# Reordering the head loop of a differential-attention decoder step across TensorE, VectorE and ScalarE

## The chip, the cores and the metric

The kernel runs on one NeuronCore of a Trainium2 chip. The metric is the device time of one execution in microseconds (us). Engines are named as in the profile: PE is TensorE (matmul), PEld its weight load, DVE is VectorE, ACT is ScalarE, POOL is GpSimd, SP is SyncE, which issues most of the loads.

## The reference

It is one inference step of a two-layer decoder, for a prompt of 512 tokens and 8 requests of 4 new tokens each (544 token columns in all), in float32. The model width is 1024. Layer 0 mixes tokens by causal pooling; layer 1 uses differential attention with 6 heads, each with two sets of 64-wide queries and keys and 128-wide values. Both layers have a small memory attention and an MLP.

```
def diff_core(q, k, v, q_pos, k_pos, lam):
    s = jnp.einsum('bqhjd,bkhjd->bhjqk', q, k) * (DIFF_HEAD_DIM ** -0.5)
    s = jnp.where(mask[None, None, None], s, NEG_INF)
    p = jax.nn.softmax(s, axis=-1)
    a = p[:, :, 0] - lam * p[:, :, 1]
    return jnp.einsum('bhqk,bkhe->bqhe', a.astype(v.dtype), v)
...
o = rmsnorm(o, p['subln'][j]) * (1.0 - lam_init)
x = x + jnp.concatenate([mix, mem_out], axis=-1) @ p['w_out'][l]
h2 = rmsnorm(x, p['norm2'][l])
x = x + jnp.square(jax.nn.relu(h2 @ p['w_mlp1'][l])) @ p['w_mlp2'][l]
```

The change touches only `diff_core` for layer 1: 24 prompt items (6 heads times 4 query blocks of 128 rows; block i sees (i+1) x 128 keys) and the 8 requests, done two at a time against 256 cached keys and 32 new ones.

## The kernel before

The kernel is one block in which each engine has its own instruction stream, ordered by hand, and the streams meet only at semaphores. Most of the time goes to 186 weight units: a 128 x 1024 slab of weights is loaded, split into a high part (ACT, L807) and a rest (DVE, L1083), and multiplied in 48 matmuls (L445). Between the value projection and the output projection of layer 1 stands the head loop, `attention(FIRST_HEAD, len(ITEMS))`, which has no weight units in it.

The loop has 28 items, numbered 20 to 47. 24 are "diff" items, called here by their width w = i+1 from 1 to 4 (keys in blocks of 128); the widths run 1, 2, 3, 4 for each head. Four are "decode" items, numbers 28, 32, 37 and 43. Items 20 to 27 are the first two heads without a decode item. The steps of an item n are these:

- scores(n), PE: two products of queries and keys (L545), or for a decode item 24 + 12 short matmuls (L556, L560). It needs the exponentials of item n-3, since the scores have three pairs of PSUM banks.
- bias(n), DVE: adds the causal mask (L1183), takes the row maximum (L1190) and scales it (L1194); for a decode item L1187, L1192 and L1198. It needs scores(n).
- exponentials(n), ACT: one or two activations with row sums (L869). It needs bias(n) and the turn of item n-3.
- weights(n), DVE: reciprocal of the sums (L1159), a ratio (L1167) and the difference of the two softmaxes (L1169); for a decode item L1172 and L1173. It needs exponentials(n).
- turn(n), PE: w transposes of the weights into PSUM bank 6 (L582); a decode item uses matmuls (L585, L587). It needs weights(n) and, since there is one such bank, the copy of item n-1.
- copy(n), ACT: bank 6 to SBUF (L883; a decode item also L882). It needs turn(n).
- mix(n), PE: w products with the values into bank 7 (L620; decode L630). It needs copy(n) and the drain of item n-1.
- drain(n), DVE: bank 7 to SBUF (L1216). A decode item needs three steps between mix and drain: a copy to SBUF on ACT (L905), a decode turn on PE (L650, `decode_turn`), then six small copies on DVE (L1222).
- clamp and squares(n) on POOL (L1623) and ACT (L893, L895), for the norm behind the attention.

After item 42 DVE also computes factors of the first 16 rows of results (L1227 to L1230 and L1236) and scales four heads (L1242), for which ACT takes a square root (L912) and must change its table of functions twice. `mix_new` (L658) adds the new tokens' share near the end. SP issues the loads of the cached keys and values of a decode item (L389), keys after the scores of the decode item before, values after its decode turn.

The order of the three streams in one turn n of the loop is: on PE scores(n+2), decode turn(n-2), turn(n), mix(n-1); on ACT exponentials(n+1), decode copy(n-2), copy(n), squares(n-3); on DVE weights(n), drain(n-2), bias(n+2). The helpers are `scores` L518, `turn` L564, `mix` L591, `decode_turn` L646 (PE), `items_exp` L860, `items_copy` L873 (ACT), `items_weight` L1151, `items_bias` L1176, `items_drain` L1201 (DVE).

Of the kernel before, what the change touches and what calls it, by code (L numbers as in the profile page):

```python
# [105 lines left out]
def build(nc, xT, memT, hist, params, consts, ropes, weights, memK, memV, cacheK, cacheV, pages,  # L106
# [5 lines left out]
    with ctx:  # L112
# [201 lines left out]
        def probs(n):  # L314
            return Pr[2 if n >= FIRST_HEAD else int(n >= L0_ITEMS)][n % slots(n)]
# [17 lines left out]
        DECODE = [n for n, it in enumerate(ITEMS) if it[0] == "decode"]  # L333

        def decode_rows(n):

            return T[:, n % 2, 4 * GROUP:4 * GROUP + 3 * P]
# [89 lines left out]
        def _(pe):  # L427
# [136 lines left out]
            def turn(n):  # L564
                kind, a, i = ITEMS[n]
                l = int(n >= L0_ITEMS)
                t0 = 6
                pr = probs(n)
                pe.wait_ge(weighted, n + 1)
                if n >= 1:  # L570
                    pe.wait_ge(copied, n)
                if kind == "mem":
                    for kt in range(2):
                        for hh in range(2):
                            at = (2 * kt + hh) * P
                            mm = pe.transpose(ps[:, t0, at:at + P], pr[:, hh, lo_of(kt)], ident)  # L576
                elif kind == "memdec":
                    for kt in range(2):
                        mm = pe.transpose(ps[:, t0, lo_of(kt)], pr[:, 0, lo_of(kt)], ident)
                elif kind == "diff":  # L580
                    for kt in range(i + 1):
                        mm = pe.transpose(ps[:, t0, lo_of(kt)], pr[:, 0, lo_of(kt)], ident)  # L582
                else:
                    for kt in range(2):
                        pe.matmul(ps[:, t0, 2 * GROUP * kt:2 * GROUP * (kt + 1)], pr[:, 0, lo_of(kt)], C2[:, n % 2, :],  # L585
                                  start=True, stop=True)
                    mm = pe.matmul(ps[0:SAMPLE, t0, 4 * GROUP:6 * GROUP], pr[:, 0, PAST:PAST + SAMPLE], C2[:, n % 2, :],  # L587
                                   start=True, stop=True)
                mm.then_inc(turned, 1)
# [72 lines left out]

            def attention(n0, n1):

                for n in range(n0, n1):
                    if n + 2 < n1:
                        scores(n + 2)
                    if n - 2 in DECODE:
                        decode_turn(n - 2)
                    turn(n)  # L670
                    if n > n0:
                        mix(n - 1)
                    if n == n1 - 1:
                        mix_new(n)
                mix(n1 - 1)
# [122 lines left out]
        def _(act):  # L798
# [98 lines left out]

            def attention(n0, n1):
                items_exp(n0)
                for n in range(n0, n1 + 3):  # L900
                    if n + 1 < n1:
                        items_exp(n + 1)
                    if n - 2 in DECODE:
                        act.wait_ge(decode_mixed, DECODE.index(n - 2) + 1)
                        act.activation(decode_rows(n - 2), ps[:, 7, 0:3 * P], ACT.Copy).then_inc(decode_copied, 1)  # L905
                    if n < n1:
                        items_copy(n)
                    if n0 <= n - 3:
                        items_square(n - 3)
                    if n == EARLY_DONE + 2:  # L910
                        act.wait_ge(sub_mean, 1)
                        act.activation(rr[:, 0:EARLY], ss[:, 0:EARLY], ACT.Sqrt, bias=eps_sub, scale=SUB)\  # L912
                           .then_inc(sub_root, 1)
# [162 lines left out]
        def _(dve):  # L1076
# [168 lines left out]
            def attention(n0, n1):  # L1245
                items_bias(n0)
                items_bias(n0 + 1)
                for n in range(n0, n1 + 2):
                    if n < n1:
                        items_weight(n)  # L1250
                    if n - 2 >= n0:
                        items_drain(n - 2)
                    if n + 2 < n1:
                        items_bias(n + 2)
                    if n == EARLY_DONE + 1:
                        dve.wait_ge(squared, EARLY)
                        means(ss[:, 0:EARLY], ss_big[:, 0:EARLY], ss[:, 0:EARLY], rr2[:, 0:EARLY], keep[:, 0:EARLY])
                    if n == EARLY_DONE + 3:
                        head_factors(0, EARLY, 1)
                        for h in range(EARLY_HEADS):  # L1260
                            scale_head(h)
                dve.wait_ge(new_mixed, 1)
                dve.wait_ge(drained, DEC[-1] + 1)
                zs = Z[:, 0:MIXT, PROMPT:TOK]
                new = ps[:, 2 * ((n1 - 2) % SLOTS), 0:NS].rearrange("p (h t) -> p h t", h=MIXT)
                dve.tensor_tensor(zs, zs, new, ALU.add).then_inc(new_added, 1)
# [477 lines left out]
```

## Time and profile before

| what | us |
|---|---|
| median of 3 runs (lowest to highest) | 1279.95 (1279.94 to 1280.48) |
| the profiled execution, its own time | 1280.49 |
| its span, first to last instruction | 1278.5 |
| head loop, first scores to the start of the last turn of heads | 717.5 to 817.4 |
| PE busy in the whole span | 1220.1 (95%) |
| mean granted TensorE clock, share of full speed | 0.977 |

The head loop takes 100 of 1278 us. The profiled execution is 0.54 us above the median and its span is 2.0 us under its own time. A profile row of the timeline gives a start and a duration, and in square brackets how long the engine stood idle before it and what ended that.

### The profile page before, as it was taken

Reading aid. Unit: us, or ns where it says so; the run is one execution under the profiler, and the core shown is the slowest. Engines: PE = TensorE matmul, PEld = TensorE weight load, DVE = VectorE, ACT = ScalarE, POOL = GpSimd, SP = SyncE. Lnnn points to the kernel's source line nnn. Section 1 sums busy time; section 2 is a strip of 40 time slices with the busy share of each in tenths; the row PEclk is TensorE's granted clock in tenths of the full one; section 3 lists DMA queues with packets and bytes.
Section 4 is the critical chain, followed back from the end, with each engine's and each line's share of the span. In section 5 each row is a group of like instructions: output and inputs, shape, how many; then the busy total and the mean of one; then the engine's idle time right before and its main releaser. Section 6 shows DMA issues by size and latency. Waiting matters only on the chain.

```text
span 1278.5 us, 23202 instructions
## 1 busy us (share of the span) xinstructions
PE 1220.1 (95%) x9578; PEld 1169.1 (91%) x9578; DVE 581.7 (45%) x880; ACT 409.2 (32%) x756; POOL 346.9 (27%) x284
## 2 busy tenths in 40 slices
PE   6998999999999999999999898699999999999997
PEld 5877999999999999998899655599999999999997
DVE  7667444333333333446635867645333333333334
ACT  6545332212212212334412456533212212211221
POOL 3363115205205205320062200012511511511521
PEclk9999999999999999999999889699999999999998
DMA  7624322222322322232354546022232232232222
GB/s 281 210 85 128 119 83 87 96 83 83 99 84 83 97 85 83 83 93 75 132 135 119 197 156 214 1 66 79 90 97 83 83 99 83 83 99 84 84 66 71
DMA packets 38032, 132.97 MB, mean 104 GB/s; under 512 B 4178, under 2 KB 7122, under 8 KB 37298
## 3 DMA queue, kind: packets, MB, share of 16 engines
q1 hardware_dynamic: 36834, 123.42, 30.5%
q0 software_dynamic: 1104, 8.15, 2.1%
q8 instruction: 76, 1.25, 0.4%
q14 instruction: 18, 0.15, 0.0%
HBM read 121.18 MB, written 7.03 MB: 100 GB/s over the span
## 4 chain that ended last, share of the span: by engine, by line
PE 89%; DVE 7%; ACT 2%; issue 1%; DMA 0%; POOL 0%; DVEq 0%; SPq 0%; ACTq 0%
PE psum L445 80%; DVE weights_split L1083 1%; DVE inv_rms L1102 1%; PE psum L620 1%; ACT weights_split L807 1%; PE psum L531 1%; PE psum L545 1%; DVE tiny L1190 1%; PE psum L582 1%; PE psum L556 1%; PE psum L602 1%; PE psum L576 0%; PE psum L630 0%; PE psum L560 0%; PE psum L490 0%
## 5 line engine op out<-in xcount | busy, mean ns | idle before, releaser
L445 PE MATMUL psum<-operand_b,weights_split 128*128 128x272 f32 x4416 | 562.6, 289 | 4.1 <-DVE weights_split L1083 3.9
L445 PEld LDWEIGHTS psum<-operand_b,weights_split 128*128 128x128 f32 x4416 | 556.7, 189 | 9.1 <-DVE weights_split L1083 4.9
L445 PE MATMUL psum<-operand_a,weights_split 128*128 128x272 f32 (+1 forms) x4068 | 521.3, 290 | 21.4 <-DVE weights_split L1083 14.8
L445 PEld LDWEIGHTS psum<-operand_a,weights_split 128*128 128x128 f32 x4068 | 514.4, 190 | 27.7 <-issue 20.3
L807 ACT ACTIVATE weights_split<-weights_raw 128x1024 fp32r<-128x1024 f32 (+1 forms) x186 | 192.6, 1036 | 395.3 <-PE psum L445 395.3
L1083 DVE TENSOR_TENSOR weights_split<-weights_raw,weights_split 128x1024 fp32r<-128x1024 f32 (+1 forms) x186 | 239.5, 1288 | 136.6 <-ACT weights_split L807 136.5
L1506 POOL TENSOR_TENSOR squares<-staging 128x544 f32<-128x544 f32 x64 | 76.5, 1195 | 469.7 <-ACT operand_a L853 207.7
L1137 DVE TENSOR_TENSOR residual<-psum,residual 128x544 f32<-128x544 f32 x48 | 34.8, 725 | 176.0 <-PE psum L445 176.0
L1118 DVE SCALAR_TENSOR_TENSOR staging<-psum,inv_rms 128x544 f32<-128x544 f32 x56 | 40.6, 724 | 150.1 <-PE psum L445 150.1
L1499 POOL TENSOR_TENSOR squares_sum<-squares_sum,squares 128x544 f32<-128x544 f32 (+1 forms) x35 | 48.6, 1389 | 115.6 <-ACT squares L819 115.0
L1508 POOL TENSOR_TENSOR operand_a<-squares,operand_a 128x544 fp32r<-128x544 f32 x32 | 64.9, 2029 | 2.5
L1508 POOL TENSOR_TENSOR operand_b<-squares,operand_b 128x544 fp32r<-128x544 f32 x32 | 64.9, 2028 | 2.5
L853 ACT ACTIVATE operand_a<-staging 128x544 fp32r<-128x544 f32 x24 | 15.8, 658 | 109.9 <-DVE staging L1118 109.9
L853 ACT ACTIVATE operand_b<-staging 128x544 fp32r<-128x544 f32 x24 | 15.8, 658 | 109.8 <-DVE staging L1118 109.8
L1106 DVE TENSOR_TENSOR residual<-psum,residual 128x544 f32<-128x544 f32 x31 | 22.5, 724 | 58.8 <-PE psum L445 58.8
L1190 DVE TENSOR_REDUCE tiny<-psum 128x2 f32<-128x512 f32 (+3 forms) x40 | 30.8, 770 | 9.9 <-PE psum L531 8.9
L819 ACT ACTIVATE squares<-residual 128x544 f32<-128x544 f32 x39 | 25.2, 646 | 30.9 <-DVE residual L1106 30.9
L814 ACT ACTIVATE operand_a<-residual,params 128x544 fp32r<-128x544 f32 x16 | 12.0, 751 | 64.1 <-DVE residual L1106 64.1
L1499 POOL TENSOR_TENSOR squares_sum<-squares 128x544 f32<-128x544 f32 (+1 forms) x6 | 8.2, 1368 | 84.1 <-ACT squares L819 84.1
L883 ACT ACTIVATE staging<-psum 128x512 f32<-128x512 f32 (+4 forms) x48 | 22.4, 468 | 26.4 <-PE psum L582 22.3
L1623 POOL TENSOR_SCALAR squares<-attention_out 128x128 f32<-128x128 f32 x24 | 7.1, 294 | 87.2 <-DVE attention_out L1216 87.2
L814 ACT ACTIVATE operand_b<-residual,params 128x544 fp32r<-128x544 f32 x24 | 17.8, 740 | 37.7 <-DVE residual L1106 37.7
(209 smaller groups left out, 729.2 us busy)
## 6 DMA issues: line engine op xcount, KB each, us to landing
weights_raw<-in_weights SPq DMA_DIRECT2D x180, 512.0 KB, 3.6
cache_tiles<-in_page_k SPq DMA_DIRECT2D x16, 384.0 KB, 4.3
cache_tiles<-in_page_v SPq DMA_DIRECT2D x16, 384.0 KB, 3.9
cache_tiles<-in_mem_k SPq DMA_DIRECT2D x8, 512.0 KB, 4.6
cache_tiles<-in_mem_v SPq DMA_DIRECT2D x8, 512.0 KB, 5.2
residual<-in_x SPq DMA_DIRECT2D x1, 2176.0 KB, 11.5
rotated<-projected POOLq DMA_DIRECT2D x4, 408.0 KB, 7.0
rotated<-keys POOLq DMA_DIRECT2D x4, 408.0 KB, 7.6
```

Of the source, the lines that this page charges most:

```text
L445: mm = pe.matmul(ps[:, 2 * (j % PS) + hf, 0:n], w(wr), act[:, ar, k, hf * n:(hf + 1) * n], start=(q == 0 and wr == 0 and ar == 0), stop=(q ...
L807: act.activation(split[:, s % HL, 0, 0:n], raw[:, s, 0:n], ACT.Copy).then_inc(weight_hi, 1)
L814: act.activation(dst, src, ACT.Copy, scale=gain(g, k)).then_inc(norm_hi, 1)
L819: act.activation(SQ[:, k % 2, 0:cols], src, ACT.Square).then_inc(sq_ready, 1)
L853: act.activation(hidden[:, 0, j, :], T[:, j % TS, :], ACT.Square).then_inc(hid_hi, 1)
L1083: dve.tensor_tensor(split[:, s % HL, 1, 0:n], raw[:, s, 0:n], split[:, s % HL, 0, 0:n].bitcast(F32), ALU.subtract).then_inc(weight_lo, 1)
L1118: dve.scalar_tensor_tensor(out=halves(T[:, j % TS, :]), in0=unit_psum(j), scalar=0.0, in1=halves(rms[:, :]), op0=ALU.max, op1=ALU.mult).th ...
L1137: dve.tensor_tensor(halves(X[:, j, :]), unit_psum(j), halves(X[:, j, :]), ALU.add)\
L1190: own.chain(dve.tensor_reduce(mx[:, s, :], sc[:, :, 0:n_keys], AX.X, ALU.max))
L1499: pool.tensor_tensor(sq_sum[:, 0:cols], a, SQ[:, k % 2, 0:cols], ALU.add).then_inc(sq_summed, 1)
L1506: pool.tensor_tensor(sq, t, t, ALU.mult).then_inc(hid_sq, 1)
L1508: pool.tensor_tensor(hidden[:, 1, j, :], sq, hidden[:, 0, j, :].bitcast(F32), ALU.subtract)\
```

## The change

It alters only the order of steps in the three `attention` loops. On PE, the scores of item n+3 come between turn(n) and mix(n-1); the scores of item n0+2 are ahead of the loop. On ACT, the exponentials of item n+2 are ahead of copy(n) and behind the decode copy of n-2. On DVE, one turn of the loop is: drain of a decode item n-2, weights(n+1), bias(n+3), drain(n-1) if that is not a decode item. No operation is added or removed.

```
@@ PE
             def attention(n0, n1):
 
+                scores(n0 + 2)
                 for n in range(n0, n1):
-                    if n + 2 < n1:
-                        scores(n + 2)
                     if n - 2 in DECODE:
                         decode_turn(n - 2)
                     turn(n)
+                    if n + 3 < n1:
+                        scores(n + 3)
                     if n > n0:
                         mix(n - 1)
@@ ACT
                 items_exp(n0)
+                items_exp(n0 + 1)
                 for n in range(n0, n1 + 3):
-                    if n + 1 < n1:
-                        items_exp(n + 1)
                     if n - 2 in DECODE:
                         act.wait_ge(decode_mixed, DECODE.index(n - 2) + 1)
                         act.activation(decode_rows(n - 2), ps[:, 7, 0:3 * P], ACT.Copy).then_inc(decode_copied, 1)
+                    if n + 2 < n1:
+                        items_exp(n + 2)
                     if n < n1:
                         items_copy(n)
@@ DVE
                 items_bias(n0)
                 items_bias(n0 + 1)
-                for n in range(n0, n1 + 2):
-                    if n < n1:
-                        items_weight(n)
-                    if n - 2 >= n0:
+                items_weight(n0)
+                items_bias(n0 + 2)
+                for n in range(n0, n1 + 1):
+                    if n - 2 in DECODE:
                         items_drain(n - 2)
-                    if n + 2 < n1:
-                        items_bias(n + 2)
+                    if n + 1 < n1:
+                        items_weight(n + 1)
+                    if n + 3 < n1:
+                        items_bias(n + 3)
+                    if n > n0 and n - 1 not in DECODE:
+                        items_drain(n - 1)
                     if n == EARLY_DONE + 1:
```

## Rows read from the trace of the kernel before

**Rows 1.** Busy time by engine in the head loop; columns as in the first line.

```profile
core 0: us, PE busy (x) PEld busy (x) DVE busy (x) ACT busy (x) POOL busy (x), PEclk, DMA share, GB/s
717.00:818.00 101.00, 82.97 (x540) 54.07 (x541) 73.43 (x229) 59.17 (x241) 12.49 (x40) 0.84 0.52 180
```

**Rows 2.** What DVE waited for in the head loop: us in total, times, longest.

```profile
DVE projected L1222 <- PE psum L650: 8.4, 4, 2.7
DVE attention_out L1216 <- PE psum L620: 7.6, 5, 4.4
DVE psum L1187 <- PE psum L560: 3.6, 3, 1.9
DVE psum L1183 <- PE psum L545: 3.1, 6, 0.8
```

**Rows 3.** The same of PE.

```profile
PE psum L582 <- DVE probs_heads L1169: 8.0, 9, 2.5
PE psum L585 <- DVE combine L1173: 2.8, 3, 1.2
...
PE psum L620 <- DVE projected L1222: 1.2, 2, 0.6
```

**Rows 4.** Timeline around the turn of decode item 37: start, duration, what.

```profile
774.76 0.49 ACT L883 ACTIVATE staging<-psum 128x384 f32<-128x384 f32 x1 [1.07 <-PE psum L582]
...
776.09 0.16 DVE L1159 RECIPROCAL tiny<-tiny 128x1 f32<-128x1 f32 x1
...
776.21 0.69 ACT L869 ACTIVATE staging<-psum,tiny 128x512 f32<-128x512 f32 x1 [0.38 <-DVE tiny L1194]
...
776.72 0.34 DVE L1216 TENSOR_SCALAR attention_out<-psum,tiny 128x128 f32<-128x128 f32 x1
776.86 0.67 PE L585 MATMUL psum<-combine,probs_heads 128*128 128x80 f32 x4 [1.22 <-DVE combine L1173]
776.89 0.68 ACT L869 ACTIVATE staging<-psum,tiny 128x512 f32<-128x512 f32 x1
```

**Rows 5.** Durations by shape of exponentials and weights, widths 1 and 4.

```profile
L869 ACT ACTIVATE probs_heads<-psum,tiny 128x128 f32<-128x128 f32 x6 | 2.1, 350 | 0.0
...
L1169 DVE SCALAR_TENSOR_TENSOR staging<-staging,tiny 128x128 f32<-128x128 f32 x3 | 1.1, 351 | 0.1
```

**Rows 6.** Timeline of the mix, copy, turn and drain of decode item 32.

```profile
763.13 2.55 PE L630 MATMUL psum<-cache_tiles,staging 128*32 128x384 f32 x16
...
765.61 0.92 PE L545 MATMUL psum<-keys,projected 64*128 64x384 f32 x4
765.76 0.49 ACT L905 ACTIVATE staging<-psum 128x384 f32<-128x384 f32 x1 [0.43 <-PE psum L630]
766.46 0.55 PE L650 MATMUL psum<-constants,staging 128*128 128x128 f32 x3
...
767.04 0.53 DVE L1222 COPY projected<-psum 128x8 f32<-128x8 f32 x6 [2.71 <-PE psum L650]
...
767.49 0.42 DVE L1183 TENSOR_TENSOR psum<-psum,constants 128x256 f32<-128x256 f32 x1
```

**Rows 7.** Timeline of the mix and copy of decode item 28.

```profile
747.98 1.50 PE L630 MATMUL psum<-cache_tiles,staging 128*32 128x384 f32 x16
...
749.48 0.58 ACT L869 ACTIVATE probs_heads<-psum,tiny 128x384 f32<-128x384 f32 x1 [0.55 <-DVE tiny L1194]
...
750.61 0.49 ACT L905 ACTIVATE staging<-psum 128x384 f32<-128x384 f32 x1
```

**Rows 8.** Busy time and clock in three stretches of 2 us; columns as in rows 1.

```profile
728.00:730.00 2.00, 2.00 (x9) 1.12 (x9) 1.61 (x6) 0.96 (x5) 0.29 (x1) 0.50 0.97 397
...
748.00:750.00 2.00, 2.00 (x33) 0.96 (x34) 1.86 (x6) 1.37 (x7) 0.00 (x0) 1.00 0.02 4
...
762.00:764.00 2.00, 2.00 (x14) 1.11 (x16) 1.66 (x6) 0.76 (x3) 0.00 (x0) 0.50 0.94 333
```

**Rows 9.** Timeline, the last mix of the loop.

```profile
814.89 2.08 PE L620 MATMUL psum<-values,staging 128*128 128x128 f32 x8
```

## The prediction

> **What bounds the kernel now.** I read the busy time of the head loop first [rows 1]. In 101 us PE is busy for 83, DVE for 73 and ACT for 59, so no engine is full: PE and DVE wait for each other in turn. The lists of waits say where. DVE stood 22.7 us: 8.4 for four decode turns, 7.6 for mixes, 3.6 and 3.1 for scores of decode and diff items [rows 2]. PE stood 8.0 + 2.8 us for the weights [rows 3]. A reordering can win back only such waits. 4.35 of the 7.6 us belong to the very last drain, behind the last mix (2.1 us, at half clock), and nothing in the change touches that [rows 2, 9]. Outside the loop nothing moves.
>
> Written as one stream, the new order is less than its name. PE went turn(n), mix(n-1), scores(n+3), turn(n+1); it will go turn(n), scores(n+3), mix(n-1), turn(n+1). DVE went weights(n), drain(n-2), bias(n+2) and will go weights(n), bias(n+2), drain(n-2). So on both engines a step moves past one neighbour. The wait of scores(n+3) for exponentials(n) is met before turn(n) can run. Only on ACT does the order bite: exponentials(n+2) used to follow copy(n) and now precede it, although they need a bias that DVE makes only after weights(n). No operation is added, so a term has a price only where the step lies on the path; I cost each with two ends.
>
> **Term A, the scores come earlier by one mix.** Bias of diff items waited 3.1 us in six places, of decode items 3.6 us in three [rows 2]. The mix now moved behind is that of item n-1. I price a mix of w products from the last one: width 4, 2.08 us at half clock, so about 1.05 at full, and 0.3 to 1.0 by width (estimate from that row) [rows 9]. The six diff waits are 0.8 us at most [rows 2] and could vanish: 3.1. Of the three decode waits the mixes in front are widths 1, 4 and 1, so 0.35 + 1.05 + 0.35, about 1.8. Upper end 4.9 us gained. Lower end: the turn in front of those scores starts later (term B) and takes it all back, 0. The half of it is nearest to what a walk through the stream gives, since PE runs at half clock in part of the first two heads [rows 8] and is then late itself: I take 2.4 us gained.
>
> **Term B, the copy waits behind the exponentials.** From the end of bias(n+2), turn(n+1) used to need drain plus weights on DVE. It now also needs exponentials(n+2), then copy(n). For the turn of item 37 the rows carry all of it: exponentials of width 4 start at 776.21 and their second part ends at 777.57, so 1.37 us; the copy of width 3 is 0.49 us; that makes 1.86 us from 776.21, and 0.1 for the semaphore [rows 4]. On DVE from the same moment, drain and decode weights in the new order are 0.27 + 0.62, and the turn follows 0.14 later: the turn of 37 came at 776.86, where the copy would allow it at about 778.1 if bias stood where it stood [rows 4]. So this turn is about 1.0 us late. For diff turns the same sum gives less. Exponentials of width 1 are 2 x 0.35 us and copies 0.28 to 0.6 us, against 0.27 + weights of 0.8 (width 1, whose last operation is 0.35) to 1.2 us (width 4) [rows 4, 5]: the turns of widths 1 and 3 are late by 0.4 to 0.5, width 2 by 0.25, width 4 not at all. Diff turns are mostly covered, for bias(n+4) comes only after bias(n+3), a drain and weights, over 2.3 us later, and turn plus scores are 1.3 to 2.0 us at full clock. If that cover is gone, at half clock, each costs up to 0.5 us. The turns of decode items are not covered where PE stood waiting for the weights, as it did three times, 2.8 us [rows 3]. The longest was 1.2, so two of them make up at least 1.6 of it. I take two turns at 1.0 us plus 0.3: 2.3 us lost; ends 0 and 4.0 (four turns) plus some 2 us for diff turns.
>
> That ACT really holds the copy back is seen in the old trace. The mix of item 28 ended at 749.48, ACT was then only about to start exponentials that had waited 0.55 us for their bias, and the decode copy came behind them at 750.61 [rows 7]. The Trainium skill, page TensorE: Matmul & The Clock Gate, section on the array of 16 x 32x32, says ScalarE and VectorE work through their queues strictly in order while TensorE can at least pull weight loads ahead. The trace agrees for ACT: 1.13 us between the end of that mix and the copy. By that rule alone term B has no way round.
>
> **Term C, the decode items.** Before, the scores of a diff item (0.85 us) stood between a decode mix and its decode turn and hid the ACT copy of 0.49 us: mix ends 765.68, turn starts 766.46, drain 767.04 [rows 6]. After, the decode turn comes straight behind the mix and PE stands while ACT copies, 0.1 + 0.5 + 0.1 = 0.65 us, and the mix itself comes 0.85 later because the scores are now ahead of it. So a decode drain comes 0.65 later, 1.95 us over three items. What is gained is that the bias that stood behind the drain (it started at 767.49, 1.5 us long; 0.8 for one item) is done within the 2.7 us for which DVE waited anyway: 1.5 + 1.5 + 0.8 = 3.8 us. The mix that stood twice for the decode drain, 1.2 us, is covered by scores now [rows 3]. But between the decode items PE has hardly a gap, and where PE is the bound the DVE gain is idle: then the term is -1.95 + 1.2 = -0.75. Ends: 0.75 lost, 1.9 gained. I take 0, nearer the PE-bound end because all three decode drains end a stretch in which PE never stops.
>
> **Term D, the end.** Weights(45) and bias(47) move ahead of the scaling of four heads, and exponentials(45) ahead of ACT's change of table, so PE can do turn(45) before the block; yet drain 43 moves behind it and mix(44) waits for that drain. One more wait for scores, at most 0.8 us [rows 2], can go there, and one decode drain is no longer waited for, at most 0.65 (term C). Ends 0 and 1.45; I take 0.6 gained, under the middle since two moves there work against each other. The last two mixes and `mix_new` stay as they are: 0.
>
> Loads: the keys of item 37 and the values of item 32 are issued after steps that come within 1 us of where they came, and both were used some microseconds after landing, so 0; if that cover went, the scores of 37 would wait under 1 us. POOL's clamp and the squares follow a drain one bias later and are used three items on: 0.
>
> **Sum.** 2.4 - 2.3 + 0 + 0.6 = 0.7 us gained. The profiled execution would go from 1280.49 to 1279.8 and, the median being 0.54 lower, the time to about 1279.3. A measurement of this kernel can tell 0.2% from no change, 2.56 us, so this is no change.
>
> **Rivals.**
> 1. *The lead pays* (faster). If PE holds its full clock, term A is there whole, C near its upper end and B small: 4.9 + 1.0 - 2.3 + 1.0 = 4.6 us, 1275.3; half way, 1276.7. For it speaks that DVE's scores waits are short and each smaller than a mix. Against it, that PE runs at half clock in parts of the loop, mean 0.84 [rows 1], just where turns and scores would have to catch up.
> 2. *Copies behind exponentials become the bound* (slower). PE idles about 2 us ahead of turns 32 and 37 (the 1.2 of before and term B's 1.0, less what it did earlier) [rows 3, 4], and the diff turns at half clock pay 0.5 each. Price: B at 5, A at 1.5, C at -0.75, D at 0.6: 3.65 lost, 1283.6. It decides from the point where exponentials plus copy (1.1 to 1.9 us) outlast drain plus weights and PE then has no slack up to the next decode drain.
> 3. *The clock* goes with either. A decode mix took 1.50 us in a stretch with the clock granted at 1.00 (2.4 GHz) and 2.55 us in one at 0.50 (1.2 GHz) [rows 6, 7, 8]; this one mix was 1.05 us longer for it. A low stretch holds two or three such steps (the turns, scores and mixes round that mix), so I estimate 2 to 3 us for one, from those two rows. One stretch less gives about 1277, one more 1282. The same page of the Trainium skill, in its section on oscillation, says idle gaps bring the low clock back; by that rule longer gaps before turns 32 and 37 speak for a slower kernel, and the shorter ones in the first heads against it. The trace agrees only in that its low stretches follow gaps.
> 4. *The change does less than its name* is my forecast itself: two swaps with a neighbour.
>
> **How the numbers follow.** Forecast, within 2.56 us: 0.47. Rival 1, with the clock's good side: 0.34. Rival 2, with its bad side: 0.19. The range from 1275.8 to 1282.8 takes in the half of rival 1 and most of rival 2; the likeliest case's own range is 1277.4 to 1281.
>
> **What would show it.** Right: DVE's waits for L545 and L560 fall from 6.7 to about 3 us; the copies L883 show waits ended by nothing, since they follow exponentials at once; PE's waits before L582 and L585 are put down to ACT L883 as well as to DVE; the decode turn L650 shows a wait for ACT L905 of about 0.65 us three times, against one before. Wrong: PE waits for L883 under 1 us in total and a loop shorter by over 3 us (rival 1), or a loop over 103 us with more than 16 us at clock 0.50 before 807 (rival 2).

## The result, and the profile after

| what | before | after |
|---|---|---|
| median on one chip, 14 executions each (lowest to highest), us | 1278.64 (1273.66 to 1280.81) | 1281.96 (1277.39 to 1286.32) |
| ratio to before, 95% interval | | 1.0031 (1.0016 to 1.0046) |
| the profiled execution, its own time, us | 1280.49 | 1283.81 |
| its span, us | 1278.5 | 1281.9 |
| head loop, us | 717.5 to 817.4, 99.9 | 718.8 to 821.9, 103.1 |

The change makes the kernel slower by 3.3 us between the medians, 4.0 us by the ratio (2.0 to 5.9). The forecast was a gain of 0.7 us, so it missed the step by 4 to 5 us and had its sign wrong. The absolute time, 1282.0, lies inside the forecast range for two reasons that are luck: the range was wide, and it started from 1279.95, the median of three executions, where 14 have 1278.64. In the tables below a ratio is an estimate from the executions and need not be the quotient of the two medians; seven executions that took at least 5% longer than the others are left out of all ratios and means.

The first two lines of the page of the profile after:

```profile
span 1281.9 us, 23202 instructions
PE 1218.9 (95%) x9578; PEld 1167.1 (91%) x9578; DVE 584.5 (46%) x880; ACT 407.7 (32%) x756; POOL 347.8 (27%) x284
```

The span is 3.4 us longer and PE's busy time is not, so PE was not given more work. The head loop by engine, with the columns of [rows 1]:

```profile
718.80:821.90 103.10, 83.15 (x537) 53.31 (x537) 74.09 (x228) 57.33 (x237) 11.68 (x39) 0.85 0.51 176
```

The same stretch of before, from its first scores to the last turn of heads:

```profile
717.50:817.40 99.90, 82.38 (x537) 53.47 (x537) 72.46 (x228) 58.62 (x237) 11.70 (x39) 0.84 0.53 182
```

Between these two profiles the loss (3.2 of 3.4 us) is in the head loop, at about the same mean clock, but more profiles will show that such a pair says little about the clock. DVE does the same 228 instructions and is busy 1.6 us longer. What DVE waited for there, against [rows 2]:

```profile
DVE psum L1189 <- PE psum L560: 10.3, 4, 5.2
DVE attention_out L1218 <- PE psum L620: 5.8, 5, 2.4
DVE projected L1224 <- PE psum L650: 3.3, 3, 1.7
DVE psum L1185 <- PE psum L545: 2.7, 5, 0.9
```

The waits for decode turns fell from 8.4 to 3.3 us, as the change of order makes them. But the waits for scores (L1185, L1189) rose from 6.7 to 13.0, where the forecast had them fall to 3. The sum of the four hardly moved: 22.1 after 22.7. So the longer loop is not in the total of DVE's listed waits. What PE waited for, against [rows 3]:

```profile
PE psum L650 <- ACT staging L905: 4.2, 4, 2.4
PE psum L556 <- DMA cache_tiles<-in_page_k: 3.4, 2, 2.1
PE psum L545 <- issue: 2.3, 2, 1.4
PE psum L620 <- DVE attention_out L1218: 2.3, 4, 1.2
PE psum L585 <- ACT staging L884: 2.2, 4, 0.9
PE psum L582 <- ACT staging L884: 2.1, 2, 1.2
PE psum L582 <- DVE probs_heads L1171: 1.9, 4, 0.6
PE psum L620 <- DVE projected L1224: 1.6, 1, 1.6
```

Three kinds of wait are new. Turns now wait 4.3 us for ACT's copy (L884), which is the mechanism of term B. The scores of decode items waited 3.4 us for their keys, which the forecast had put at nothing. And four mixes waited 2.3 us for the drain of a diff item (L1218), which now stands behind a bias; no term of the forecast had this. The timeline of after, at the scores of item 32 and the mix of item 28, and further down at the weights of item 43:

```profile
751.33 1.92 PE L556 MATMUL psum<-cache_tiles,query_blocks 128*32 128x256 f32 x24 [2.15 <-DMA cache_tiles<-in_page_k]
...
754.64 1.50 PE L630 MATMUL psum<-cache_tiles,staging 128*32 128x384 f32 x16
...
756.20 0.49 ACT L905 ACTIVATE staging<-psum 128x384 f32<-128x384 f32 x1 [4.34 <-PE psum L630]
...
756.75 0.55 PE L650 MATMUL psum<-constants,staging 128*128 128x128 f32 x3 [0.61 <-ACT staging L905]
...
801.23 0.16 DVE L1196 SCALAR_TENSOR_TENSOR tiny<-tiny 128x2 f32<-128x2 f32 x1
801.31 0.34 DVE L1218 TENSOR_SCALAR attention_out<-psum,tiny 128x128 f32<-128x128 f32 x1
...
801.76 0.16 DVE L1161 RECIPROCAL tiny<-tiny 128x1 f32<-128x1 f32 x1
...
803.64 0.34 DVE L1218 TENSOR_SCALAR attention_out<-psum,tiny 128x128 f32<-128x128 f32 x1
...
803.91 0.16 DVE L1229 TENSOR_SCALAR tiny<-tiny 128x16 f32<-128x16 f32 x1
```

The upper four rows show the wait for keys and term C's 0.61 us between a decode mix and its turn. The lower rows hold what the forecast overlooked, and one has to read starts to see it, since no bracket stands there. Behind a drain of 0.34 us (L1218) the next operation starts 0.27 us later when it is L1229 (803.64 to 803.91), but 0.45 us later when it is the reciprocal of the weights (801.31 to 801.76).

The reason is a wait in `items_weight`, lines 1156 to 1161 of after:

```
s, pr = n % SLOTS, probs(n)
...
dve.wait_ge(exped, n + 1)
if n >= FIRST_HEAD + SLOTS:
    dve.wait_ge(drained, n - SLOTS + 1)
own.chain(dve.reciprocal(coef[:, s, 0:nj], sums[:, s, 0:nj]))
```

Reciprocals and ratios have three slots. Weights(n) overwrite those of item n-3, so they wait until drain(n-3) is complete, and DVE makes that drain itself. In the old order a whole bias stood between drain(n-3) and weights(n), so the wait was long met. In the new order that drain is the instruction just ahead. DVE then waits for its own last instruction, 24 times in the loop, where the kernel before does so once (at weights(47)): 23 x 0.18 = 4.1 us more. Call this **theory C**. It was formed only when the first two batches of runs had left the loss without a cause. Their expectations know only of the other two, **theory A**, the copies behind the exponentials (that is term B, larger than forecast), and **theory B**, the wait for the keys. The letters of the theories are not those of the terms.

### The profile page after: what moved, and what is told of

It reads as the page before. It is cut to its first block, busy times and chain, and to the rows that moved or that the text cites. A ratio compares the mean times of both kernels' runs of the same rounds, so it can differ in the third digit from the quotient of the medians.

```text
span 1281.9 us, 23202 instructions
## 1 busy us (share of the span) xinstructions
PE 1218.9 (95%) x9578; PEld 1167.1 (91%) x9578; DVE 584.5 (46%) x880; ACT 407.7 (32%) x756; POOL 347.8 (27%) x284
## 4 chain that ended last, share of the span: by engine, by line
PE 88%; DVE 6%; ACT 2%; issue 1%; DMA 1%; SPq 1%; POOL 0%; DVEq 0%; ACTq 0%
PE psum L445 80%; DVE weights_split L1085 1%; DVE inv_rms L1104 1%; PE psum L620 1%; DMA cache_tiles<-in_page_k 1%; ACT weights_split L808 1%; PE psum L545 1%; PE psum L531 1%; PE psum L556 1%; PE psum L602 1%; PE psum L560 1%; DVE tiny L1192 1%; PE psum L576 0%; PE psum L490 0%; PE psum L582 0%
## 5 line engine op out<-in xcount | busy, mean ns | idle before, releaser
L445 PE MATMUL psum<-operand_a,weights_split 128*128 128x272 f32 (+1 forms) x4068 | 522.0, 290 | 21.9 <-DVE weights_split L1085 14.6
L1512 POOL TENSOR_TENSOR squares<-staging 128x544 f32<-128x544 f32 x64 | 76.4, 1193 | 470.0 <-ACT operand_b L854 207.7
L1108 DVE TENSOR_TENSOR residual<-psum,residual 128x544 f32<-128x544 f32 x31 | 22.5, 725 | 58.3 <-PE psum L445 58.3
L620 PEld LDWEIGHTS psum<-values,staging 128*128 128x128 f32 x120 | 18.8, 229 | 13.2 <-issue 7.4
```

Of the source, the lines that this page charges most:

```text
L445: mm = pe.matmul(ps[:, 2 * (j % PS) + hf, 0:n], w(wr), act[:, ar, k, hf * n:(hf + 1) * n], start=(q == 0 and wr == 0 and ar == 0), stop=(q ...
L620: mm = pe.matmul(ps[:, m0, 0:P], pt[:, lo_of(kt)], Vt[:, kt, a * P:(a + 1) * P], start=(kt == 0), stop=(kt == i))
L1512: pool.tensor_tensor(sq, t, t, ALU.mult).then_inc(hid_sq, 1)
```

## The experiments

Each ratio is to the kernel before, run beside it on the same chip, with its 95% interval; each batch has its own before.

### One engine's new order at a time

`act_back` leaves PE and DVE in the new order and puts ACT back:

```
@@ ACT
-                items_exp(n0 + 1)
                 for n in range(n0, n1 + 3):
+                    if n + 1 < n1:
+                        items_exp(n + 1)
                     if n - 2 in DECODE:
...
-                    if n + 2 < n1:
-                        items_exp(n + 2)
```

> The changed order on PE and DVE, the old order on ACT (exponentials n+1, then the copy of n). Theory A, copies behind exponentials are the loss: the waits of L582 and L585 for the copy L884 (4.3 us in the changed kernel) go, and the kernel is level with the one before or up to 2 us faster. Theory B, the decode scores ahead of the mix meet the load of the cached keys and PE idles: the wait of L556 for the load stays at 2 to 4 us or grows, since PE arrives there earlier still, and the kernel stays 2 to 4 us above the one before.

Measured: 1280.21 us, ratio 1.0026 (1.0007 to 1.0044), before 1278.03. No turn waits for the copy any more, and the kernel stays slower. By the time alone that is what theory B expected (2 to 4 us above before), though PE waited only 1.6 us for keys. By net time ACT's order is at most a small part of the loss; that it does two opposite things is seen further down. The next three make one engine's part of the diff alone, first ACT's:

> Only ACT has the changed order (exponentials n+2 ahead of the copy of n), PE and DVE as before. Theory A: 2 to 4 us slower than before, with PE waiting for L884 by 3 us or more. Theory B: ACT's order costs under 1 us, PE does not wait for the load of keys, and the kernel is within 1 us of the one before.

Measured: 1285.30 us, ratio 1.0060 (1.0039 to 1.0081). PE's waits for the copy, in the list of waits of this kernel:

```profile
PE psum L585 <- ACT staging L883: 6.5, 4, 2.5
PE psum L582 <- ACT staging L883: 6.5, 6, 2.8
```

13.0 us of such waits come with 7.7 us of lost time, about twice what theory A expected. So the mechanism of term B is real and dear when PE and DVE keep their old order. With all three engines in the new order 4.3 us of these waits are left. The likely reason, not tested by itself, is that DVE's new order makes the bias earlier for which the exponentials wait.

PE's part alone:

> Only PE has the changed order (scores n+3 between the turn of n and the mix of n-1). DVE still drains n-2 ahead of bias n+2, so it waits for a mix that now comes behind scores. Theory A: no loss from it, 0 to 1 us. Theory B: slower by 2 to 4 us; L556 waits for the load of keys, or the drains L1216 and L1222 wait for the mix by several us more than the 16.0 us of before.

Measured: 1282.12 us, ratio 1.0037 (1.0019 to 1.0054). The waits of DVE for mixes and decode turns:

```profile
DVE attention_out L1217 <- PE psum L620: 14.9, 13, 2.2
DVE projected L1223 <- PE psum L650: 8.2, 4, 3.9
```

The mix comes later by one scores step, the drain waits for it, and bias stands behind the drain: 7.6 us of waits for mixes have become 14.9. PE waited 1.1 us for keys here.

DVE's part alone:

> Only DVE has the changed order (bias n+2 ahead of the drain of n-2). PE has the mix ahead of the scores, so the bias waits a little longer, but decode drains no longer stand ahead of a bias. Theory A and theory B both have it without a loss: within 1.5 us of before, with the waits of L1222 down from 8.4 us and those of L1187 up. If it is 2 us or more slower, the DVE order itself is a third cause: PE's mix waits for a late drain.

Measured: 1317.94 us, ratio 1.0324 (1.0296 to 1.0353), far outside of what any theory expected.

```profile
DVE psum L1183 <- PE psum L545: 29.8, 17, 3.6
DVE psum L1187 <- PE psum L560: 15.9, 4, 4.4
PE psum L620 <- DVE attention_out L1216: 14.8, 14, 2.0
PE psum L620 <- DVE projected L1222: 8.4, 4, 4.7
```

The two engines wait for each other in turn. PE, in its old order, does scores(n+3) behind mix(n-1), and that mix needs drain(n-2). DVE, in its new order, does drain(n-2) only behind bias(n+2), and bias(n+3) needs scores(n+3). So bias, drain, mix and scores run one after another in every turn of the loop. DVE waits for PE and PE for DVE, 68.9 us in these four rows. DVE's and PE's parts only make sense together.

### The keys

`after_small` and `before_small` load 8 columns of the keys of decode items 32, 37 and 43 where 768 are loaded otherwise; the scores of these items are then made from older keys in the rest of the columns.

```
-    sp.dma_start(kv[:, s, part, g * 768:(g + 1) * 768], pages_part[page])
+    w = 8 if part == 0 and n != DEC[4] else 768
+    sp.dma_start(kv[:, s, part, g * 768:g * 768 + w], pages_part[page][:, 0:w])
```

> The changed kernel, but the loads of cached keys for decode items 32, 37 and 43 move 8 columns instead of 768, so these items' scores are made from keys left in the buffer. Theory B (scores reach PE before the keys): the wait of L556 for the load, 3.4 us, is gone, and with it the half-clock stretch behind it; 3 to 5 us faster than the changed kernel, level with the one before. Theory A (copies behind exponentials): 1 us faster at most, since DVE and PE then wait elsewhere; still 2 us or more above the one before.

> The kernel before, with the same shortened loads (the same part of the scores made from old keys). It did not wait for keys, so both theories have it within 1 us of the kernel before. If it gains 2 us or more, the keys' traffic costs something else than a wait, and that has to be taken off the result of the other one.

> The kernel before, unchanged, as a null run and for a second profile of its head loop. The ratio should be 1.000 within 0.15%; the loop 99.9 us long within 1.5 us. If the loop's length varies by more, one profile can't tell the versions apart and only the timed runs count.

> The changed kernel again, beside the others. The ratio should lie within 1.0016 to 1.0046 as in the first timing, and a second profile should show the loop at 103.1 us within 1.5 us, PE waiting for the load of keys by 2 to 4 us and for copies L884 by 3 to 5 us. If the key wait is absent this time and the time is the same, theory B falls.

Measured, before at 1278.19:

| kernel | median us | ratio | wait for keys in its profile, us |
|---|---|---|---|
| after, small key loads | 1283.96 | 1.0041 (1.0024 to 1.0059) | 0 |
| after, again | 1283.27 | 1.0031 (1.0013 to 1.0049) | 0.2 |
| before, small key loads | 1277.45 | 0.9993 (0.9973 to 1.0013) | 0 |
| before, again | 1276.84 | 0.9991 (0.9973 to 1.0010) | 0 |

Theory B falls twice: taking the loads away wins nothing, and in its second profile the changed kernel waited only 0.2 us for keys and was as slow. The null run shows how far one profile can be trusted: the loop of before took 96.0 us here, at a mean clock of 0.89, against 99.9 at 0.84 in the first profile, where 1.5 us of difference were expected at most. Loop lengths of single profiles differ by more than the effect that is sought.

One figure scatters less: DVE's own time in the loop, its length less all that the list of waits gives for DVE there. It stands in the table behind the next batches.

### Four slots for theory C

`coef4` is the changed kernel with a fourth slot, so that weights(n) wait for drain(n-4), which is long done:

```
-        tiny = new("tiny", [P, 164])
+        tiny = new("tiny", [P, 172])
...
-                s, pr = n % SLOTS, probs(n)
+                s, pr = n % CO, probs(n)
...
-                if n >= FIRST_HEAD + SLOTS:
-                    dve.wait_ge(drained, n - SLOTS + 1)
+                if n >= FIRST_HEAD + CO:
+                    dve.wait_ge(drained, n - CO + 1)
```

with `CO = 4`, and the same index in `items_drain`.

> The changed kernel with four slots instead of three for the reciprocals and ratios, so weights(n+1) wait for the drain of n-3 and not for that of n-2, the instruction just ahead of them on DVE. Theory C (DVE waits for its own last instruction): the start of L1161 comes 0.27 us behind the start of the drain L1218 instead of 0.45, DVE's stream is 23 times 0.18 = 4.1 us shorter, and the kernel is 1.5 to 3.5 us faster than the changed one (ratio 1.0005 to 1.0020). Theory A (copies behind exponentials alone): no change, ratio 1.0025 to 1.0040.

Measured: 1279.56 us, ratio 1.0005 (0.9989 to 1.0022), before 1278.45. The timeline of this kernel at the weights of item 43, the place shown above for after:

```profile
796.08 0.16 DVE L1198 SCALAR_TENSOR_TENSOR tiny<-tiny 128x2 f32<-128x2 f32 x1
796.15 0.34 DVE L1220 TENSOR_SCALAR attention_out<-psum,tiny 128x128 f32<-128x128 f32 x1
796.41 0.15 DVE L1163 RECIPROCAL tiny<-tiny 128x1 f32<-128x1 f32 x1
```

Its head loop by engine:

```profile
718.70:815.40 96.70, 80.50 (x538) 51.24 (x538) 72.35 (x228) 57.22 (x237) 11.71 (x39) 0.88 0.54 188
```

The reciprocal follows the drain after 0.26 us, DVE is busy 72.35 us as in before (72.46), and most of the loss is gone, as theory C expected. Two kernels build on it: `back_coef4` has ACT's old order too, and `back_coef4_turn` does turn(n) ahead of the decode turn of n-2, to hide the 0.65 us of term C:

```
@@ PE
+                    turn(n)
                     if n - 2 in DECODE:
                         decode_turn(n - 2)
-                    turn(n)
```

> The same, and ACT in its old order. Theories A and C together: both losses gone, ratio 0.998 to 1.001, no wait of L582 or L585 for the copy. If it stays above 1.002, a third cause in PE's order is left: the decode turn behind the ACT copy, 0.6 us four times.

> The same, and on PE turn(n) ahead of the decode turn of n-2, so that the ACT copy of a decode item has a turn to hide behind. Third cause real: L650's wait for the decode copy falls from 4.0 to about 3 us (the one at the change of table stays) and 0.5 to 1.5 us are gained on the one before it; ratio 0.997 to 1.000. Third cause absent: within 0.5 us of it.

Measured: 1277.81 us, ratio 1.0002 (0.9982 to 1.0022), and 1278.61 us, ratio 0.9997 (0.9976 to 1.0017). Neither beats before by anything that can be measured. PE waited 3.6 us for keys in the profile of `back_coef4` (that execution took 1281.47 us), more than in the first profile of after, and by its median the kernel is still level with before. The turn in front does hide what it should: in `back_coef4` decode turns waited 4.0 us for ACT, here

```profile
PE psum L652 <- ACT staging L908: 1.7, 4, 0.8
```

but the two kernels can't be told apart by their times, so what the 0.65 us are worth is not shown. `before_selfwait` puts the suspected wait into the kernel before, where weights(n) stand behind bias(n+1):

```
                     if n < n1:
+                        if n0 < n < n1 - 1:
+                            dve.wait_ge(biased, n + 2)
                         items_weight(n)
```

> The kernel before with one wait more: ahead of weights(n), DVE waits for the end of the last operation of bias(n+1), which is the instruction just ahead of it. Only this cost is added, some 0.18 us 26 times = 4.7 us of DVE's stream. Theory C: 1.5 to 4 us slower than the kernel before (ratio 1.0012 to 1.0030), L1159 starting some 0.27 us behind L1194 instead of 0.08. Theory A: no effect, ratio within 0.999 to 1.001.

Measured: 1279.11 us, ratio 1.0004 (0.9984 to 1.0025), under what theory C expected. But the wait itself is smaller than the expectation had it, 0.19 us from start to start and not 0.27, where a reciprocal follows 0.08 us behind the last operation of a bias otherwise. First this kernel, then before:

```profile
790.15 0.15 DVE L1198 TENSOR_SCALAR tiny<-tiny 128x1 f32<-128x1 f32 x1
790.34 0.17 DVE L1159 RECIPROCAL tiny<-tiny 128x2 f32<-128x2 f32 x1
```

```profile
797.16 0.16 DVE L1194 SCALAR_TENSOR_TENSOR tiny<-tiny 128x2 f32<-128x2 f32 x1
797.24 0.17 DVE L1159 RECIPROCAL tiny<-tiny 128x2 f32<-128x2 f32 x1
```

So the dose was about 25 x 0.11 = 2.7 us of DVE's time and not 4.7. All of it paid would be a ratio of 1.0021, and that lies inside the interval. This run neither shows nor excludes that the old order pays for such a wait.

### The same again, and the dose doubled

With one test for theory C and one that gave no answer, after and `coef4` ran again on another chip, with a third kernel, the changed one with a second wait of DVE for itself in each turn:

```
                     if n + 3 < n1:
+                        dve.wait_ge(weighted, n + 2)
                         items_bias(n + 3)
```

> The changed kernel, to stand on the same chip and in the same rounds as the next two. Ratio 1.0015 to 1.0045.

> The changed kernel with four slots, timed beside the changed one. Theory C: 1.5 to 4 us under it. If it lies within 1 us of it, the first gain was drift between chips, theory C has only a small part, and the clock or the order of PE holds the rest.

> The changed kernel with the disputed cost doubled: DVE also waits for the end of weights(n+1), the instruction just ahead, before bias(n+3), some 0.19 us 25 times = 4.7 us of DVE's stream. Theory C (in the new order DVE's stream is on the path, so each such wait is paid): 2 to 4.5 us slower than the changed kernel, ratio 1.005 to 1.007. If it costs under 1 us, as the like wait did in the old order, DVE's stream is not on the path in the new order either and theory C falls.

Measured, before at 1276.83: after 1282.12 us, ratio 1.0040 (1.0021 to 1.0058); `coef4` 1279.40, ratio 1.0014 (0.9996 to 1.0031); the doubled wait 1280.64, ratio 1.0024 (1.0008 to 1.0040). The gain of the fourth slot is there again, 2.7 us. The second wait shows in the timeline, 0.39 us between two operations that stand 0.27 apart otherwise. First this kernel, then after:

```profile
799.22 0.35 DVE L1171 SCALAR_TENSOR_TENSOR staging<-staging,tiny 128x128 f32<-128x128 f32 x1
799.61 0.43 DVE L1185 TENSOR_TENSOR psum<-psum,constants 128x256 f32<-128x256 f32 x1
```

```profile
804.85 0.35 DVE L1171 SCALAR_TENSOR_TENSOR staging<-staging,tiny 128x128 f32<-128x128 f32 x1
805.12 0.42 DVE L1185 TENSOR_TENSOR psum<-psum,constants 128x256 f32<-128x256 f32 x1
```

That is 0.12 us each and not 0.19, so the dose is not doubled but raised by at most 25 x 0.12 = 3.0 us. Still the whole is 1.5 us under after where 2 to 4.5 us more were expected. As a test of dose it failed, and by the words of its expectation theory C falls in one part: it is not so that every such wait of DVE is paid at the end of the kernel.

The table puts the profiles side by side; each line is one profile. "Own" is the length of the loop less DVE's waits.

| kernel | loop | DVE waits | DVE own | DVE busy | clock | ratio |
|---|---|---|---|---|---|---|
| before | 99.9 | 23.5 | 76.4 | 72.5 | 0.84 | |
| before, again | 96.0 | 19.9 | 76.1 | 72.2 | 0.89 | 0.9991 |
| after | 103.1 | 22.9 | 80.2 | 74.1 | 0.85 | 1.0031 |
| after, second | 100.9 | 20.3 | 80.6 | 74.3 | 0.84 | 1.0031 |
| after, third | 99.2 | 18.2 | 81.0 | 74.5 | 0.86 | 1.0040 |
| `coef4` | 96.7 | 20.3 | 76.4 | 72.4 | 0.88 | 1.0005 |
| `coef4`, second | 96.4 | 20.0 | 76.4 | 72.4 | 0.89 | 1.0014 |
| `act_back` | 97.0 | 16.8 | 80.2 | 73.9 | 0.88 | 1.0026 |
| `before_selfwait` | 95.9 | 16.8 | 79.1 | 74.3 | 0.89 | 1.0004 |
| doubled wait | 98.4 | 15.5 | 82.9 | 75.7 | 0.88 | 1.0024 |
| after, small key loads | 100.5 | 19.7 | 80.8 | 74.2 | 0.86 | 1.0041 |
| before, small key loads | 92.8 | 16.8 | 76.0 | 72.1 | 0.93 | 0.9993 |
| `back_coef4` | 98.7 | 23.3 | 75.4 | 71.5 | 0.91 | 1.0002 |

DVE's own time is 76.0 to 76.4 us in the order of before, 80.2 to 81.0 in the new order with its wait, and 75.4 to 76.4 with four slots. The difference fits the 23 x 0.18 = 4.1 us, and every profile shows it. How much of it reaches the end is another question. DVE's waits for others don't answer it: they are 15.5 to 16.8 us with the wait put into the old order or with a second one, but also 16.8 in `act_back` and in before with small key loads.

Four stretches between starts of weights(n) narrow it down, in us (the values of several profiles, where there are several):

| stretch | before | after | `coef4` | before with wait | doubled wait | `act_back` |
|---|---|---|---|---|---|---|
| 20 to 28, no decode item | 21.0 to 21.9 | 23.0 to 23.2 | 22.4 to 22.6 | 22.45 | 23.89 | 22.5 |
| 28 to 40, three decode items | 42.5 to 43.6 | 43.5 to 47.6 | 43.1 to 43.3 | 41.5 | 42.1 | 41.4 |
| 40 to 44, full clock | 11.03 | 11.61 | 11.40 | 11.28 | 11.93 | 11.60 |
| 44 to 47, the end | 11.31 | 10.66 | 9.90 | 11.18 | 10.73 | 12.01 |

In the first two heads, and in 40 to 44, which repeats to some hundredths from profile to profile, every added wait costs time, the doubled one too. Between the decode items single profiles can't tell: before with small key loads took 39.7 us there, 3 to 4 us less than the other two profiles of that order.

### The clock of all executions

Every timed execution has its mean granted clock on record, and there are enough of them to compare. In the 121 executions of before that were timed beside the other kernels, 0.001 less of clock goes with 0.87 us more of time (correlation -0.90). The next table sets the mean clock of each kernel against that of before beside it, and the difference of the mean times against what the clock would make by this slope.

| kernel | clock, before | clock, this | lost, us | with the clock | rest |
|---|---|---|---|---|---|
| after, again | 0.9825 | 0.9782 | 4.6 | 3.7 | 0.9 |
| after, small key loads | 0.9825 | 0.9768 | 5.1 | 5.0 | 0.1 |
| after, third | 0.9835 | 0.9778 | 5.4 | 4.9 | 0.4 |
| `coef4` | 0.9823 | 0.9824 | 1.0 | 0.0 | 1.0 |
| `coef4`, second | 0.9835 | 0.9822 | 2.1 | 1.1 | 1.0 |
| doubled wait | 0.9835 | 0.9814 | 3.8 | 1.8 | 2.0 |
| `before_selfwait` | 0.9823 | 0.9815 | 0.9 | 0.8 | 0.1 |
| `act_back` | 0.9828 | 0.9816 | 2.6 | 1.1 | 1.5 |

The changed kernel was granted a lower clock in each of these three timings, on two chips, once with small key loads. Between 1.2 and 2.4 GHz a mean that is 0.004 to 0.006 lower is 11 to 15 us more of the span at the lower level. Most of its loss comes with that, and the fourth slot, which takes 2.7 to 3.3 us away beside it on one chip, takes away most of the difference in clock and nothing of the rest. The doubled wait has the largest rest among the kernels with the new order, but a better clock than after, and so a shorter time. These are estimates: within 37 executions of the changed kernel (the first timing among them, mean clock 0.9791) the slope is 0.66 and not 0.87, which would put a quarter less to the clock. They also don't say which comes first, since the clock could fall for longer waits of PE, or the waits could grow because matmuls take longer at the lower level.

## Why the prediction was wrong

**The step that failed** is in term B: "on DVE from the same moment, drain and decode weights in the new order are 0.27 + 0.62". The 0.27 is the distance of a drain to the bias behind it, which does not wait for it. In the new order weights stand there, and they do wait for it: 0.45. The forecast followed data from engine to engine and took a step on one engine as free to stand behind any other. The slot that weights(n) overwrite, and the wait that guards it, stood in the kernel and in no term. Taking the wait away took the ratio from 1.0031 to 1.0005 (timed on different chips) and from 1.0040 to 1.0014 (side by side), about 3 us each time, so it is the larger part of the loss. By the estimates of the last table the price reached the end mostly together with a lower clock, and not simply as 23 x 0.18 us added up. The rest, 0.6 and 1.8 us over before in these two timings, is at the edge of what was measured.

**Term A** (2.4 us gained) was not earned. DVE's waits for scores were 13.0, 8.8 and 8.9 us in three profiles of after, and 6.7 and 6.0 in two of before, where the forecast had them fall to about 3. Being one mix ahead did not bring the scores earlier for DVE, since DVE asks for them earlier too: weights(n+1) and bias(n+3) no longer have a drain between them. In 40 to 44 the new order is slower even with four slots (11.40 against 11.03). A price that the forecast left out altogether may be in this: drain(n-1) now stands behind bias(n+3), and mix(n) needs that drain. PE waited for drains of diff items 2.3, 2.9 and 2.9 us in the three profiles of after and 2.9 in both of `coef4`, at four mixes each, and never in two profiles of before. No run took this wait away, so its price is not shown. By the lower end of term A, 0, the sum would have been 1.7 us lost, close to the 0.6 and 1.8 of `coef4`; that agreement may be chance.

**Term B** (2.3 us lost) is there as a wait, 4.3 us in all, and named right: ACT L884. Two turns of decode items waited 0.92 us each, near the 1.0 of the forecast, but two diff turns of the first heads waited 1.15 and 0.90, where all diff turns together were put at 0.3. What the waits cost in time no run isolates. Putting ACT back won 0.05% on after and 0.03% on `coef4`, each well inside its interval, but it also undid term D: 44 to 47 took 12.01 us in `act_back` against 10.66 (and 11.55 in `back_coef4` against 9.90), since in `act_back` DVE then waited 1.5 us for exponentials and PE 3.2 us for the decode drain instead of 1.6. So the small net gain probably hides a larger price of the copies. Alone, with the old order of PE and DVE, ACT's part costs 7.7 us, beyond the upper end of 6.

**Term C** (0) is as described. The decode turn waits about 0.6 us for ACT three times, and DVE's wait for decode turns fell by 5.1 us. Hiding the 0.6 us won nothing that could be measured.

**Term D** (0.6 gained) is right: 44 to 47 took 11.31 us before and 10.66 after, and ACT's new order makes it.

**The loads**: "the scores of 37 would wait under 1 us" was too low. In the first profile of after they waited 1.22 us and those of item 32 waited 2.15; in the other two all waits for keys were 0.2 and 1.5 us. It is not the cause.

**The rivals.** The second, slower, is on the right side with the right size (1283.6, itself outside the stated range), but the mechanism that it names, ACT, is not what the fourth slot took away. Its sign, a loop over 103 us, was there in the first profile (103.1) and not in two others (100.9 and 99.2), and the other half of the sign, more than 16 us at clock 0.50 before 807, the kernel before shows too (about 21 us). The third, the clock, was priced at 2 to 3 us for one more stretch at the lower level, about 1282. Over all executions it is what most of the loss comes with, but the forecast had no step in the new order from which a lower clock would follow. In single profiles it also blurs each look: a wait for keys and a half-clock stretch fell together in the first profile of after. The stretch of that profile in which the scores of item 37 ran, with the columns of [rows 1]:

```profile
772.00:774.00 2.00, 2.00 (x10) 1.03 (x6) 0.00 (x0) 0.00 (x0) 0.00 (x0) 0.50 0.92 280
```

and those scores in the timeline:

```profile
770.49 2.79 PE L556 MATMUL psum<-cache_tiles,query_blocks 128*32 128x256 f32 x24 [1.22 <-DMA cache_tiles<-in_page_k]
...
773.21 2.77 PE L560 MATMUL psum<-keys,query_blocks 128*128 128x32 f32 x12
```

5.5 us for the scores of one decode item at 1.2 GHz, and DVE waits 5.2 of them. That is half of the 10.3 us in the list of DVE's waits, and it is one execution's.

**What stays open** is why DVE's wait for itself in the new order goes with a lower clock, and why a second such wait on top of it came with a higher one and a shorter time (0.9814 against 0.9778, 1.5 us less). The table of clocks says by what way the loss is carried, not what sets it off. Open too is the rest of about 1 us that both timings of `coef4` have at the clock of before, for which the late drains and the copies are candidates, and whether the old order pays for such a wait at all.

## What to carry to other kernels

Before two steps on one engine change places, list every semaphore that either waits for, those that guard the reuse of a small slot too, and look whether its producer now stands just ahead: another slot is cheap. Where single profiles of the same kernel differ by more than the effect, compare what scatters less, here an engine's own time (a stretch less its listed waits) and starts of the same step at full clock, and compare the mean clocks of all timed executions before calling the clock noise. And an order of several engines is one thing: ACT's part of this change alone cost twice what the whole cost, and DVE's part alone ten times.

## What the runs showed of the hardware

A wait of DVE for the instruction just ahead on DVE is not free and hardly shows in the list of waits (none of the 24 in after does). From start to start, with it and without: 0.45 and 0.27 us behind a drain of 0.34 us, 0.39 and 0.27 behind an operation of 0.35, 0.79 and 0.67 behind one of 0.75, 0.19 and 0.08 behind one of 0.16. So it costs 0.11 to 0.18 us each. The Trainium skill, page VectorE: DVE Perf Modes, section "The DRAIN you can't avoid", says of a chain of copies that a semaphore after each "costs nothing extra"; for these short operations the trace disagrees, and the measurement decides.

The granted clock of the loop differs from execution to execution of one kernel: before had a mean of 0.84 in one profile and 0.89 in the next, and the loop was 3.9 us shorter in the second, with the same instructions. Over 121 executions of before, 0.001 of the mean clock of the whole span goes with 0.87 us. And an order of steps can shift the mean itself: 0.9768 to 0.9791 in four timings of the changed order, 0.9822 and 0.9824 in two of the same order with a fourth slot.
